# Three down projections by seven block products in place of eight, in four of their eleven row-chunk pairs

## What is computed

```
def _swiglu(t, w_gate, w_up, w_down):
    return (jax.nn.silu(t @ w_gate) * (t @ w_up)) @ w_down
# t: 256 x 1024, w_gate and w_up: 1024 x 2816, w_down: 2816 x 1024
h = h + 0.5 * _rmsnorm(f, ffn_post_g[l])
```

## Time and profile before

| what | value |
|---|---|
| median of three runs | 1840.99 us |
| the profiled execution | 1840.98 us, its span 1839.2 us |
| TensorE busy | 1828.7 us, 99% of the span, 10945 matmuls |
| VectorE busy | 1287.4 us, 70% |
| ScalarE busy | 1091.1 us, 59% |
| GpSimd busy | 205.6 us, 11% |
| granted TensorE clock | 1.000 over the span |

### The profile page before, as it was taken

One profiled execution on the slowest core, in us unless ns is written; L12 is line 12 of the kernel. 1 busy time (PEld: TensorE's weight loads), 2 busy tenths in 40 slices (PEclk: granted clock), 3 DMA queues, 4 the chain that ended last, 5 costly groups with the idle time before them and its releaser, 6 DMA issues.

```text
span 1839.2 us, 28833 instructions
## 1 busy us (share of the span) xinstructions
PE 1828.7 (99%) x10945; PEld 1634.4 (89%) x10945; DVE 1287.4 (70%) x2046; ACT 1091.1 (59%) x1888; POOL 205.6 (11%) x158
## 2 busy tenths in 40 slices
PE   9999999999999999999999999999999999999998
PEld 7888999998888888889999888888889998989997
DVE  7775747787777567755777778755768765768764
ACT  7664545555666466645555657655557654757653
POOL 0220001110022002200111102210002210001210
PEclk9999999999999999999999999999999999999999
DMA  8775575555576557655654548654747665537663
GB/s 247 217 218 182 172 193 162 149 154 185 171 223 188 191 154 224 192 193 139 197 170 141 194 145 230 188 195 145 222 138 214 190 196 154 173 115 207 198 193 103
DMA packets 436041, 333.87 MB, mean 182 GB/s; under 512 B 25402, under 2 KB 381504, under 8 KB 435904
## 3 DMA queue, kind: packets, MB, share of 16 engines
q1 hardware_dynamic: 435440, 331.57, 60.2%
q10 hardware_dynamic: 464, 0.47, 0.1%
HBM read 330.91 MB, written 1.05 MB: 180 GB/s over the span
## 4 chain that ended last, share of the span: by engine, by line
PE 97%; DVE 2%; ACT 1%; DMA 0%; issue 0%; SPq 0%; ACTq 0%
PE bank L1831 16%; PE bank L1808 15%; PE bank L1810 15%; PE bank L1809 15%; PE bank L1819 7%; PE bank L1833 7%; PE bank L1820 7%; PE bank L1821 7%; PE bank L1837 2%; PE bank L1830 1%; DVE wlo L1150 1%; PE bank L2120 0%; PE bank L2186 0%; PE bank L2157 0%; PE bank L2191 0%; DVE U L1203 0%
## 5 line engine op out<-in xcount | busy, mean ns | idle before, releaser
L1150 DVE TENSOR_TENSOR wlo<-raw,whi 128x1024 fp32r<-128x1024 f32 (+2 forms) x634 | 757.2, 1202 | 288.9 <-ACT whi L600 279.6
L600 ACT ACTIVATE whi<-raw 128x1024 fp32r<-128x1024 f32 (+2 forms) x634 | 642.8, 1023 | 324.8 <-PE bank L1810 247.0
L1831 PE MATMUL bank<-U,whi 128*128 128x512 f32 x1280 | 439.2, 395 | 0.0
L1833 PE MATMUL bank<-U,wlo 128*128 128x256 f32 x1120 | 314.6, 281 | 0.0
L1819 PE MATMUL bank<-U,whi 128*128 128x256 f32 x1024 | 289.2, 282 | 0.0
L1820 PE MATMUL bank<-U,whi 128*128 128x256 f32 x1024 | 286.1, 279 | 0.0
L1821 PE MATMUL bank<-U,wlo 128*128 128x256 f32 x1024 | 286.0, 279 | 0.0
L1831 PEld LDWEIGHTS bank<-U,whi 128*128 128x128 f32 x1280 | 230.2, 188 | 42.5 <-issue 0.2
L1808 PE MATMUL bank<-whi,hhi 128*128 128x512 f32 x560 | 219.3, 392 | 0.0
L1808 PE MATMUL bank<-whi,U 128*128 128x384 f32 (+2 forms) x592 | 219.1, 370 | 0.1
L1810 PE MATMUL bank<-wlo,hhi 128*128 128x512 f32 x560 | 218.1, 390 | 0.0
(11 more groups left out here) (314 smaller groups left out, 2376.6 us busy)
## 6 DMA issues: line engine op xcount, KB each, us to landing
raw<-in_ffn_w_up SPq DMA_DIRECT2D x351, 256.0 KB, 3.5
raw<-in_ffn_w_down SPq DMA_DIRECT2D x264, 256.0 KB, 2.9
raw<-in_ffn_w_gate SPq DMA_DIRECT2D x175, 256.0 KB, 3.4
raw<-in_w_gate SPq DMA_DIRECT2D x128, 192.0 KB, 2.9
raw<-in_w_in SPq DMA_DIRECT2D x80, 256.0 KB, 3.5
raw<-in_a_w_in SPq DMA_DIRECT2D x48, 256.0 KB, 3.2
raw<-in_w_mem_kv SPq DMA_DIRECT2D x32, 256.0 KB, 3.4
raw<-in_w_out SPq DMA_DIRECT2D x32, 256.0 KB, 3.0
```

What stands on the lines that cost most here:

```text
L600: act.activation(whi[n % SLOTS][:, 0:w], raw[n % RAW][:, 0:w], ACT.Copy).then_inc(hi_ready, 1)
L1150: dve.tensor_tensor(wlo[n % SLOTS][:, 0:w], raw[n % RAW][:, 0:w], whi[n % SLOTS][:, 0:w].bitcast(F32), ALU.subtract).then_inc(lo_ready, 1)
L1831: ins = pe.matmul(dst, wh, u2[:, k, :], start=(k == 0), stop=(k == KT - 1))
L1833: pe.matmul(dst[:, 0:TOK], wl, uhi[:, k, :], start=False, stop=False)
```

## The change

In three of the four down projections (f = 1, 2, 3), four of the eleven pairs of row chunks (pairs 2, 4, 6 and 8) are no longer multiplied as 2 x 2 blocks with eight block products, but in the form with seven products (Winograd's form of Strassen's scheme). The two token blocks and the two hidden tiles of a pair are the blocks of the left side, the two chunks of the pair and their two column halves those of the right side. Each product is still made in three parts.

For this the hidden sums (four tiles of 128 x 128 for each pair) are made on VectorE, rounded on ScalarE and their rest written by GpSimd, during the gate and up phase. The weight sums (four of 128 x 512 for each pair) are made by GpSimd from the raw slots in three instructions, and split by ScalarE and VectorE like two more chunks; of the pair's first chunk only one half is split. So a pair has the chunks e (512 wide), o, s (two sums) and t (two sums). The raw slots of e and o may be loaded again only when GpSimd has read them too. Some products accumulate in banks 0 to 3 over the four pairs; ten VectorE instructions (`fold`) add them into banks 4 to 7 ahead of the tail, in which TensorE waits for each bank. The raw slots become one tile so that a sum can read across two of them, and some semaphores are merged to make room.

```diff
 # SyncE, load
+                if before_it is not None:
+                    sp.wait_ge(lo_ready, halves_done(before_it))
+                    if ck.sums_before_reload(before_it):      # e: 3x+1, o: 3x+3
+                        sp.wait_ge(wsum_done, ck.sums_before_reload(before_it))
 # GpSimd, ffn
+                    if f and n % 2 == 0 and n // 2 - 1 in SEVEN:
+                        pool.wait_ge(ahi_done, x + 1)
+                        pool.tensor_tensor(alo[:, x % NS, :, :], asum[:, :, :], ahi[:, x % NS, :, :].bitcast(F32), ALU.subtract)
...
+                if f:
+                    for q in SEVEN:
+                        weight_sums(seven_of(f, q))
+            def weight_sums(x):
+                e = ck.seven[x]
+                for c in (e, e + 1):
+                    pool.wait_ge(w_loaded[ck.slot(c)], ck.loads(c))
+                if x:
+                    pool.wait_ge(lo_ready, halves_done(ck.seven[x - 1] + 3))
+                    pool.wait_ge(folded, 10 * (x // NS))
+                at = ck.slot(e) * CW
+                pool.tensor_tensor(wsum[:, 0:2, :].rearrange("p a n -> p (a n)"), raw_all[:, at + 512:at + 512 + CW], raw_all[:, at:at + CW],
+                                   ALU.subtract).then_inc(wsum_done, 1)
+                odd = raw[ck.slot(e + 1)]
+                pool.wait_ge(wsum_done, 3 * x + 1)
+                pool.tensor_tensor(wsum[:, 2, :], odd[:, half[0]], wsum[:, 0, :], ALU.subtract).then_inc(wsum_done, 1)
+                pool.wait_ge(wsum_done, 3 * x + 2)
+                pool.tensor_tensor(wsum[:, 3, :], odd[:, half[1]], wsum[:, 2, :], ALU.subtract).then_inc(wsum_done, 1)
 # ScalarE, split_to: chunk s waits for 3x+1 weight sums, chunk t for 3x+3
+                    if n in ck.sums:
+                        act.wait_ge(wsum_done, 3 * ck.sums[n][0] + (3 if ck.sums[n][1] else 1))
 # ScalarE, ffn: one more copy of 128 x 512 for each pair
+                        act.wait_ge(asum_done, 4 * x + 4)
+                        act.activation(ahi[:, x % NS, :, :], asum[:, :, :], ACT.Copy).then_inc(ahi_done, 1)
 # VectorE, ffn
+                    if f and n % 2 and n // 2 in SEVEN:
+                        hidden_sums(seven_of(f, n // 2), i)     # four tensor_tensor of 128 x 128
...
+                else:
+                    fold(f)
+                split_to(n0 + ffn_chunks(f) - TAIL - 1 + SLOTS)
+            def fold(f):
...
+                split_to(e + 5)
+                dve.wait_ge(w_used, e + 1)
+                dve.wait_ge(lo_ready, halves_done(e + 3))
+                dve.tensor_copy(wsum[:, 0, :], bank[0][:, :]).then_inc(folded, 1)
+                split_to(e + 6)
+                dve.wait_ge(w_used, e + 2)
+                dve.wait_ge(folded, done + 1)
+                into_bank(4, 0)          # bank[4] = bank[4] + wsum[0]
+                split_to(e + 7)
+                dve.wait_ge(w_used, e + 3)
+                add_bank(2, 2, 0)        # wsum[2] = bank[2] + wsum[0]
+                add_bank(1, 3, 0)
+                dve.wait_ge(w_used, e + 4)
+                dve.wait_ge(folded, done + 4)
+                add_bank(1, 1, 1)
+                dve.wait_ge(folded, done + 5)
+                into_bank(5, 1)
+                add_bank(2, 1, 2)
+                dve.wait_ge(folded, done + 7)
+                into_bank(6, 2)
+                add_bank(3, 3, 2)
+                dve.wait_ge(folded, done + 9)
+                into_bank(7, 3)
 # TensorE
+            def seven_products(f, q):
...
+                start_chunk(e)
+                product(0, hhi[:, even, ts[0]], hlo[:, even, ts[0]], e, half[0], start, stop).then_inc(w_used, 1)
+                start_chunk(o)
+                product(4, hhi[:, odd, ts[0]], hlo[:, odd, ts[0]], o, half[1], False, stop)
+                pe.wait_ge(alo_done, x + 1)
+                product(5, *hidden_sum(3), o, half[0], False, stop).then_inc(w_used, 1)
+                start_chunk(sums)
+                product(3, *hidden_sum(0), sums, half[0], start, stop)
+                product(2, *hidden_sum(2), sums, half[1], start, stop).then_inc(w_used, 1)
+                start_chunk(ends)
+                product(1, *hidden_sum(1), ends, half[0], start, stop)
+                product(6, hhi[:, odd, ts[1]], hlo[:, odd, ts[1]], ends, half[1], False, stop).then_inc(w_used, 1)
...
+                def bank_ready(t, nb):
+                    pe.wait_ge(folded, 10 * (f - 1) + (2, 6, 8, 10)[2 * t + nb])
```

More of the change, by code:

```diff
@@ L39 @@
 GROUPS = FF // 256
+SEVEN = (2, 4, 6, 8)
+NS = len(SEVEN)
 VB = 344
@@ L93, in __init__ @@
         self.narrow = {}
+        self.raw = {}
+        self.loaded = []
+        self.sums = {}
+        self.seven = []
     def take(self, n, width=CW):
@@ L97, in take @@
         self.count += n
+        for c in range(first, first + n):
+            self.raw[c] = len(self.loaded)
+            self.loaded.append(c)
         if width != CW:
@@ L101, in take, with take_seven, slot, loads @@
         return first
+    def take_seven(self):
+        x = len(self.seven)
+        first = self.take(1, CW // 2)
+        self.take(1)
+        assert self.raw[first] % 2 == 0
+        for n in range(2):
+            self.sums[self.count] = (x, n)
+            self.count += 1
+        self.seven.append(first)
+        return first
     def width(self, c):
         return self.narrow.get(c, CW)
+    def slot(self, c):
+        return self.raw[c] % RAW
+    def loads(self, c):
+        return 32 * (self.raw[c] // RAW + 1)
+    def last_in_slot(self, c):
+        return self.loaded[self.raw[c] - RAW] if self.raw[c] >= RAW else None
+    def sums_before_reload(self, c):
+        if c in self.seven:
+            return 3 * self.seven.index(c) + 1
+        if c - 1 in self.seven:
+            return 3 * self.seven.index(c - 1) + 3
+        return 0
 def program(nc, A, consts, out):
@@ L385, in sides, with rows_of @@
                 return pieces
-            def rows_of(w, k):
+            def rows_of(w, k, swap=False):
                 def pieces(slot):
-                    return [(slot[:, half[nb]], w[k * P:(k + 1) * P, half[nb]]) for nb in range(2)]
+                    return [(slot[:, half[1 - nb if swap else nb]], w[k * P:(k + 1) * P, half[nb]]) for nb in range(2)]
                 return pieces
@@ L1866, in token_block, with down_rows, tail @@
                 return ins
-            def down_rows(c, t, nb, first, xh, xl, k, start, stop):
-                return moving3(bank[first + 2 * t + nb][:, :], xh[:, k, ts[t]], xl[:, k, ts[t]], c, half[nb], start, stop)
-            def tail(c, n, first, xh, xl, full, turns, ready=None):
+            def down_rows(c, t, nb, first, xh, xl, k, start, stop, resumed=False):
+                return moving3(bank[first + 2 * t + nb][:, :], xh[:, k, ts[t]], xl[:, k, ts[t]], c, half[nb], start, stop, resumed)
+            def tail(c, n, first, xh, xl, full, turns, ready=None, bank_ready=None):
                 at = n - TAIL
                 for nb in range(2):
+                    if bank_ready:
+                        bank_ready(0, nb)
                     for j in range(at, n):
```

181 lines of the change are left out of this document (130 added, 51 removed).

## The result

The changed kernel takes 1847.02 us (median of 7 runs, 1846.36 to 1847.78) against 1840.99: a ratio of 1.0034, 95% interval 1.0024 to 1.0043. It is 6 us slower (0.34%, more than the 0.2% that can be told here) and 1.0 us above the forecast. The profiled execution has a span of 1845.1 us, 5.9 more than before.

A forecast was written before the change was run, and what follows sets the result against it. TensorE, busy 99%, was taken to bound the kernel. Later transposes in three projections (1.5 + 0.8 + 1.5 = 3.8 us) plus 1.2 us for semaphore waits, on 1841.0, gave 1846 us; own range 1842 to 1852, overall 1837.5 to 1856.

The forecast's parts named there:

- The loop of the sums: GpSimd's weight sums in the down projection come round every 10.7 us (8.4 to 12.8) against TensorE's 10.2.
- the last third sum: Last changed pair's third weight sum on GpSimd ends 41.4 us after the first down matmul (33.6 to 47.6).
- a pair's sums: GpSimd's three weight sums: 4.98 us alone plus about 1.3 us waiting for VectorE's splits, 6.3 us.
- the wait for o: Between pairs, GpSimd waits 4.4 us for the next chunk o's reload and low part (3.4 to 5.6).
- the third rival: Loop of sums takes 11.6 to 12.8 us, 8 to 18 us on top, 1854 to 1864; chance 0.10.
- The fold and the tail: VectorE's end chain stalls TensorE 2.0 us at bank 4; first transpose 1.5 us later, 0.8 in f = 2.
- The 1.2 us for semaphore waits: Estimated addition for waits of 0.05 to 0.1 us at some six places of each loop of sums.
- the fourth rival: TensorE's clock falls to 1.2 GHz after the tail stall: 8 to 16 us on top, 1850 to 1860; chance 0.07.
- the signs of being wrong: Sums round in under 10.2 us, ten fold ops under 5.5 us, TensorE stalling in the gate phase, or a lower clock.
- the gate phase: Hidden sums on VectorE, ScalarE's copy and GpSimd's rest (1.34 us) fit in idle time: no cost taken.
- The first rival: Weight sums in time, only the fold counts: transpose at 56.8, 1.9 us gained in all, 1839 us; chance 0.25.

The follow-up runs named there:

- e4: Changed kernel with the first pair's three weight sums moved ahead of GpSimd's last two hidden rests: 1844.00 us, ratio 1.0011 to the kernel before.
- e7: Changed kernel with three pairs by seven products (groups 2, 5 and 8) in place of four: 1848.76 us, ratio 1.0044 to the kernel before.
- e8: Changed kernel; ScalarE copies bank 0, GpSimd makes two low parts, the first addition precedes a tail split: 1842.36 us, ratio 1.0007 to the kernel before.

## Why the prediction came out right

**The loop of the sums** was forecast at 10.7 us and measured at 10.9, and the last third sum at T = 41.4 and 41.78. Its parts were each off, in opposite directions: a pair's sums take 7.1 to 7.3 us from the second pair on (forecast 6.3), since the third meets a split as well, and the wait for o is 3.5 to 3.7 us (forecast 4.4, lower bound 3.4). That the two errors, 0.9 and 0.8 us, cancel was luck in the sum as it was set up: with the sums at 7.2 and the wait at 4.4 us it would have been 11.6, the third rival's loop. The rows of VectorE above suggest why they go together: it has the same 5.5 low parts to make in a loop, whether between the sums or behind them. The prediction did not use that. Its end of the first pair's sums is also added up a little low: 3.4 + 2.40 + 1.29 + 1.08 + 1.29 is T = 9.5, not 9.2; measured 9.3. That the loop is above 10.2 because of the exclusion is shown by the constant writes; that its lateness is the loss, by the thin sums.

**The fold and the tail.** Bank 4 was to be ready at T = 48.3 and TensorE to stall 2.0 us. `into_bank` ended at 653.95, T = 48.75, and the stall was 2.55. From the end of t's low part (649.34) to there it is 4.61 us against 4.68 in the sum; the 0.5 us come from the late start of the chain. Its later part kept that distance: `post_norm`'s first add ends at T = 59.08, forecast 58.6. The ten instructions of the fold take 6.6 us there, forecast 6.5. The 1.2 us for semaphore waits, 0.4 in each projection, cover the 0.5: 1.96 where 1.5 + 0.4 was forecast, in f = 1 and f = 3. That is luck in part: six places in each of nine loops at 0.05 to 0.1 us would be 2.7 to 5.4 us, and no run measures these waits by themselves.

**The size that was off is f = 2:** 0.8 + 0.4 us forecast, 1.70 measured. VectorE's add ends there at 851.37 us and the transpose starts at 851.86, not 0.06 later as in f = 1 (664.28, 664.34); TensorE itself is late, because of its clock. Windows of the changed kernel, three of f = 1, one of f = 2 and one of f = 3 (PE, PEld, DVE, ACT and POOL busy, granted clock, DMA share, GB/s):

```profile
651.00:654.00 3.00, 0.66 (x3) 0.19 (x2) 3.00 (x5) 0.87 (x1) 0.00 (x0) 1.00 0.70 207
654.00:657.00 3.00, 2.80 (x8) 2.26 (x9) 2.90 (x4) 1.74 (x2) 0.00 (x0) 0.63 0.99 311
657.00:660.00 3.00, 3.00 (x13) 2.37 (x12) 2.90 (x6) 1.07 (x3) 0.00 (x0) 0.80 0.54 185
844.00:847.00 3.00, 3.00 (x10) 2.34 (x10) 2.83 (x6) 0.41 (x1) 0.00 (x0) 0.68 0.34 113
1267.00:1270.00 3.00, 2.90 (x12) 2.17 (x12) 2.86 (x5) 1.55 (x2) 0.00 (x0) 1.00 0.92 301
```

Behind the 2.55 us stall the granted clock falls to the lower level, 1.2 GHz, for about 3 us in f = 1 and f = 2 (the fourth row): matmuls start 0.43 us apart instead of 0.227. In f = 3, after the same stall, it stays at 1.00. So the fourth rival's event came, with a chance of 0.07, but not its price of 8 to 16 us: VectorE is the late one there, and the slow matmuls fill the time in which TensorE would have waited for bank 5 (a wait of 0.69 us in f = 3 and none in f = 1 and f = 2). Only f = 2 shows a cost, 0.4 us. The seven runs bear that out: their mean granted clock is 0.996 to 0.998 and does not order their times (1847.30 us at 0.998, 1846.53 at 0.997). Of the signs of being wrong that the prediction lists, this is the one that came.

**Also as forecast:** the gate phase has no new stall of TensorE, although GpSimd's low part of the hidden sums took 2.26 us and not 1.34, and ScalarE hides its copy. The first rival's time (1839, T = 56.8) is what the kernel would take with sums in time: 1840.0 and 1840.1 us, T = 56.85. Its gain in f = 2 was worked out as 1.1 us and is 1.0 (T = 56.16).

**What I had not seen** is how little an earlier start gives (e4), and that a longer distance between pairs gives nothing (e7). Both came from taking the loop as GpSimd's alone, where VectorE's low parts, slots of TensorE and the order on ScalarE close it too.

## What to carry to other kernels

When work moves to an idle engine, draw the loop that it closes, not its busy time: its input's slot, the in-order queue behind its output, the reload and the engine that it excludes decide the period. Here the period was some 0.6 us over that of TensorE, the engine that bounds the kernel, and this was lost once a turn until the stage ended. GpSimd's sums and VectorE's low parts, both with two SBUF inputs, stop each other, so price both as if on one engine wherever they overlap: here 11.2 us by that sum, 10.8 measured. Saved matmuls are paid out only if the last chain of the stage (here splits, fold and normalization on VectorE) is shortened as well: here 8.2 us of matmuls turned into a loss of 6 us, and into a gain of 3.6 once the sums were earlier and the chain shorter.

## What was not expected of the hardware

TensorE's clock fell after some stalls and not after others of the same length. Of the stalls ahead of the tail in the changed kernel, e4 and e7, those of 2.55 and 2.55 (changed), 2.00 (e4, f = 2) and 2.25 us (e7, f = 1) were followed by a granted clock of 0.60 to 0.68 in a stretch of 3 us; those of 2.54 (changed, f = 3), 3.15 and 1.83 us (e7, f = 2 and 3) by 1.00. After those of 0.7 to 1.3 us in e4 and e8 it stayed at 1.00. What tells the two kinds apart stays open. The Trainium skill, TensorE: Matmul & The Clock Gate (Part 1), takes the lower clock as the resting state that activity releases. The runs agree so far: from 10 us of the span to the last matmul of the ten profiled executions, the clock falls only behind the four stalls named first. They also show that a stall of this size may bring it or may not.
